# Keys of both head pairs first, then values 512 columns wide over two halves of the depth

## The reference

```
h_ctx = modulate(rms_norm(ctx), ...)             # 256 context tokens
h     = modulate(rms_norm(x), ...)               # 512 tokens
k_ctx, v_ctx = split(h_ctx @ w_in[:, 512:1536])  # 4 heads of 128
s_f = einsum('bhld,hl,bhle->bhde', k_ctx, w_f, v_ctx)   # decayed states, forward
s_b = einsum('bhld,hl,bhle->bhde', k_ctx, w_b, v_ctx)   # and backward
q, k, v, g, f = split(h @ w_in)                  # 512 columns each
q, k = rope(q), rope(k)
o = retention(q, k, v, forward, s_f) + retention(q, k, v, backward, s_b)
```

## Time and profile before

| | |
|---|---|
| time, median of 3 runs | 1349.7 us (1349.34 to 1349.88) |
| profiled execution, its own time | 1348.56 us |
| its span, first to last instruction | 1346.8 us |
| TensorE matmul busy | 1327.9 us, 99% of the span |
| VectorE busy | 901.4 us, 67% |
| ScalarE busy | 526.4 us, 39% |
| GpSimd busy | 83.8 us, 6% |
| 16 DMA engines, mean | 131 GB/s |
| granted TensorE clock, mean | 1.000 |

### The profile page before, as it was taken

One profiled execution on the slowest core, in us unless ns is written; L12 is line 12 of the kernel. 1 busy time (PEld: TensorE's weight loads), 2 busy tenths in 40 slices (PEclk: granted clock), 3 DMA queues, 4 the chain that ended last, 5 costly groups with the idle time before them and its releaser, 6 DMA issues.

```text
span 1346.8 us, 15738 instructions
## 1 busy us (share of the span) xinstructions
PE 1327.9 (99%) x6461; PEld 1077.6 (80%) x6461; DVE 901.4 (67%) x1126; ACT 526.4 (39%) x747; POOL 83.8 (6%) x148
## 2 busy tenths in 40 slices
PE   7999999999999999999999999999999999999998
PEld 4799688778888888887888777778878888888886
DVE  4787878988777777678758899766875433332224
ACT  4552444344334443222422666774333222222112
POOL 0000001000000001010000100000002220000000
PEclk9999999999999999999999999999999999999999
DMA  9543046324445555654123211112224332224331
GB/s 390 191 141 126 17 155 220 125 78 175 163 162 196 171 183 186 217 202 173 71 94 98 90 64 63 63 63 96 98 86 131 116 115 94 94 98 161 107 104 63
DMA packets 32887, 176.47 MB, mean 131 GB/s; under 512 B 4128, under 2 KB 4400, under 8 KB 17840
## 3 DMA queue, kind: packets, MB, share of 16 engines
q1 hardware_dynamic: 19440, 128.78, 26.7%
q0 software_dynamic: 13376, 46.69, 10.8%
HBM read 171.26 MB, written 4.20 MB: 130 GB/s over the span
## 4 chain that ended last, share of the span: by engine, by line
PE 90%; DVE 5%; issue 2%; ACT 2%; DMA 2%; SPq 0%; DVEq 0%; ACTq 0%
PE bank L1475 27%; PE bank L1477 26%; PE bank L1476 26%; PE bank L1814 2%; PE bank L1815 2%; PE bank L1820 2%; PE bank L1680 1%; DMA adaf<-ada 1%; PE bank L2010 1%; PE bank L1980 1%; DVE WL L830 1%; DVE sums L1174 1%; PE bank L1998 1%; PE bank L1997 1%; DMA raw<-weights 1%
## 5 line engine op out<-in xcount | busy, mean ns | idle before, releaser
L1475 PE MATMUL bank<-hH,WH 128*128 128x512 f32 x992 | 390.1, 393 | 0.9 <-DVE WL L830 0.6
L830 DVE TENSOR_TENSOR WL<-raw,WH 128x2048 fp32r<-128x2048 f32 x103 | 234.5, 2278 | 230.2 <-ACT WH L372 230.2
L1477 PE MATMUL bank<-hH,WL 128*128 128x512 f32 x992 | 386.4, 390 | 0.0
L1476 PE MATMUL bank<-hL,WH 128*128 128x512 f32 x992 | 386.2, 389 | 0.0
L372 ACT ACTIVATE WH<-raw 128x2048 fp32r<-128x2048 f32 x106 | 201.5, 1904 | 237.3 <-DMA raw<-weights 237.3
L1475 PEld LDWEIGHTS bank<-hH,WH 128*128 128x128 f32 x992 | 186.3, 188 | 42.6 <-issue 3.3
L1477 PEld LDWEIGHTS bank<-hH,WL 128*128 128x128 f32 x992 | 186.2, 188 | 39.6
L1476 PEld LDWEIGHTS bank<-hL,WH 128*128 128x128 f32 x992 | 186.3, 188 | 37.6 <-issue 0.2
L859 DVE SCALAR_TENSOR_TENSOR ada_acc<-ada_half,csil,ada_acc 128x1024 f32<-128x1024 f32 x70 | 89.7, 1281 | 6.4 <-DMA ada_half<-ada_later 3.8
L1307 DVE SCALAR_TENSOR_TENSOR cacc<-uT,vec,cacc 128x511 f32<-128x511 f32 (+29 forms) x120 | 83.3, 755 | 0.0
L335 POOL DMA_DIRECT2D ada_half<-ada_later x80 | 42.4, 530 | 571.8 <-DVE ada_acc L859 333.4
(11 more groups left out here) (333 smaller groups left out, 2075.1 us busy)
## 6 DMA issues: line engine op xcount, KB each, us to landing
raw<-weights SPq DMA_DIRECT2D x108, 1024.0 KB, 4.9
ada_half<-ada_later POOLq DMA_DIRECT2D x80, 512.0 KB, 4.4
adaf<-ada SPq DMA_DIRECT2D x8, 1024.0 KB, 19.8
xT<-x_t SPq DMA_DIRECT2D x4, 512.0 KB, 5.7
x_rows<-xB POOLq DMA_DIRECT2D x32, 64.0 KB, 2.2
x_tok<-x_rows POOLq DMA_DIRECT2D x1, 2048.0 KB, 10.9
out_t<-x_tok SPq DMA_DIRECT2D x8, 256.0 KB, 2.0
ctxT<-ctx_t SPq DMA_DIRECT2D x1, 1024.0 KB, 28.6
```

Source lines behind the costliest of these rows:

```text
L830: TT_(WL[:, slot, 0:width], raw[:, slot, 0:width], WH[:, slot, 0:width], sub).then_inc(s.lo_done, 1)
L1475: mm(o, lh, rh, start=start, stop=False, skip_group_check=skip)
L1476: mm(o, lh, rl, start=False, stop=False, skip_group_check=skip)
L1477: return mm(o, ll, rh, start=False, stop=stop, skip_group_check=skip)
```

## The change

Chunk order and layout: the four chunks after the queries were keys 0, values 0, keys 1, values 1. They are now keys 0, keys 1 and two chunks of values (`C_VALUES` and the next), each with all 512 value columns of one half of the depth (512 of the 1024 input rows). The values are therefore made with 512 moving columns: per token block 4 x 3 matmuls from the first chunk and 4 x 3 from the second into the same bank, in place of 2 pairs x 8 x 3 matmuls of 256 columns.

TensorE's new list: keys 0 (banks 6, 7), context keys 0 (banks 4, 5), keys 1 (banks 0, 1), context keys 1 (banks 2, 3), first half of the values (tokens into banks 6, 7, 4, 5, context into 0, 1), second half: context first, then token blocks 2 and 3, then `states(0)` into bank 0, then token blocks 0 and 1; then the retention loop, where `states(1)` goes into bank 1. Scores 0 and 1 now wait for the copies of token blocks 2 and 3 (`v_read`).

```
-                pe.wait_ge(s.rope_sum, HEADS)
-                states(0)
...
+            have(C_VALUES)
+            for t in range(TT):
+                pe.wait_ge(s.rope_sum, HEADS + t + 1) if t < 2 else pe.wait_ge(s.kc_scaled, t - 1)
+                value_part(0, VALUE_BANKS[t], hH, hL, t)
+            for tt in range(TC):
+                pe.wait_ge(s.rope_sum, HEADS + 2 + tt + 1)
+                ins = value_part(0, tt, hcH, hcL, tt)
+            ins.then_inc(s.mm_done, 16)
+            have(C_VALUES + 1)
+            for tt in range(TC):
+                value_part(1, tt, hcH, hcL, tt).then_inc(s.mm_done, step(tt, TC + TT))
+            for x, t in enumerate(VALUE_ORDER):
+                if x == 2:
+                    states(0)
+                value_part(1, VALUE_BANKS[t], hH, hL, t).then_inc(s.mm_done, step(TC + x, TC + TT))
...
+                    else:
+                        pe.wait_ge(s.v_read, i + 1)
...
-                    pe.wait_ge(s.state_lo, 1)
                     states(1)
                     pe.wait_ge(s.v_read, 4)
```

VectorE's new list (`context_keys` holds the same instructions per pair as before, `value_tile` is one copy of 128x512 in place of one of the four copies before):

```
+            rope_pair(0, KEY_BANKS[0], kH, kL, C_KV, 4, HEADS)
+            split_lo(C_VALUES)
+            context_keys(0)
+            rope_pair(1, KEY_BANKS[1], kH, kL, C_KV + 1, 4, HEADS)
+            split_lo(C_VALUES + 1)
+            ada_steps(2)
+            context_keys(1)
+            ada_steps(2)
+            for tt in range(TC):
+                dve.wait_ge(s.vc_hi, tt + 1)
+                TT_(vcL[:, tt, :], bank[tt][:, :], vcH[:, tt, :], sub).then_inc(s.vc_lo, 1)
+            dve.wait_ge(s.kc_lo, 4)
+            dve.wait_ge(s.places_in, 32)
+            decay_args(0)
+            split_lo(C_F)
...
+            ada_steps(2)
+            value_tile(0)
+            value_tile(1)
+            ada_steps(2)
+            states_lo(0)
+            value_tile(2)
+            value_tile(3)
```

More of the change, by code:

```diff
@@ L85 @@
 BAND = L + (TT - 1) * P
+KEY_BANKS, CONTEXT_BANKS, VALUE_BANKS = (6, 0), (4, 2), (6, 7, 4, 5)
+VALUE_ORDER = (2, 3, 0, 1)
+C_VALUES = C_KV + 2
 HALF, FOLD = L // 2, L // 2 + 2
@@ L115, in build @@
         rstd = fix("rstd", [P, L])
+        SCRATCH_AT = base[0]
         scratch = fix("scratch", [P, 2, L])
@@ L452, in states_hi @@
                 A(sH[:, :, 2 * p:2 * p + 2, :],
-                  bank[3][:, :].rearrange("p (d h e) -> p d h e", d=2, h=2), ACT.Copy).then_inc(s.state_hi, 1)
+                  bank[p][:, :].rearrange("p (d h e) -> p d h e", d=2, h=2), ACT.Copy).then_inc(s.state_hi, 1)
             def decays(h):
@@ L471, in _, with context_keys_hi @@
             A(csdH[:, :], csd_in[:, :], ACT.Copy).then_inc(s.csd_hi, 1)
[L473 to L480, removed]
+            def context_keys_hi(p):
                 for tt in range(TC):
                     act.wait_ge(s.kc_scaled, 2 * p + tt + 1)
[L483 to L490, removed]
+                    A(kcH[p][:, tt, :, :], kctmp[:, :, :], ACT.Copy).then_inc(s.kc_hi, 1)
+            rope_pair(0, KEY_BANKS[0], kH, C_KV, 4, HEADS)
+            split_hi(C_VALUES)
+            context_keys_hi(0)
+            rope_pair(1, KEY_BANKS[1], kH, C_KV + 1, 4, HEADS)
+            split_hi(C_VALUES + 1)
+            context_keys_hi(1)
+            for tt in range(TC):
+                act.wait_ge(s.mm_done, done(C_VALUES + 1, tt, TC + TT))
+                A(vcH[:, tt, :], bank[tt][:, :], ACT.Copy).then_inc(s.vc_hi, 1)
+            decays(0)
+            split_hi(C_F)
+            states_hi(0)
             def token_decays(h):
@@ L994, in _, with context_keys @@
             TT_(csdL[:, :], csd_in[:, :], csdH[:, :], sub).then_inc(s.csd_lo, 1)
[L995 to L1006, removed]
+            def context_keys(p):
                 for tt in range(TC):
-                    dve.wait_ge(s.mm_done, done(C_KV + 2 * p, 2 + tt, 4))
+                    dve.wait_ge(s.mm_done, done(C_KV + p, 2 + tt, 4))
                     if 2 * p + tt:
@@ L1016, in _, with value_tile @@
                     dve.wait_ge(s.kc_hi, 2 * p + tt + 1)
[L1017 to L1033, removed]
+                    TT_(kcL[p][:, tt, :, :], kctmp[:, :, :], kcH[p][:, tt, :, :], sub).then_inc(s.kc_lo, 1)
+            rope_pair(0, KEY_BANKS[0], kH, kL, C_KV, 4, HEADS)
[13 more added lines that the diff above has]
+            split_lo(C_F)
+            def value_tile(x):
+                t = VALUE_ORDER[x]
+                dve.wait_ge(s.mm_done, done(C_VALUES + 1, TC + x, TC + TT))
+                V.tensor_copy(vF[:, t, :], bank[VALUE_BANKS[t]][:, :]).then_inc(s.v_read, 1)
+            ada_steps(2)
[5 more added lines that the diff above has]
+            value_tile(3)
             def cross(h):
@@ L1593, in _, with states @@
                     turn(c)
+            def states(q):
+                pe.wait_ge(s.kc_lo, 2 * q + 2)
+                pe.wait_ge(s.vc_lo, TC)
+                for d in range(2):
+                    for h in range(2):
+                        at = slice(P * (2 * d + h), P * (2 * d + h) + P)
+                        hs, vs = slice(P * h, P * h + P), slice(256 * q + P * h, 256 * q + P * h + P)
+                        for tt in range(TC):
+                            ins = mm3(bank[q][:, at], kcH[q][:, tt, d, hs], kcL[q][:, tt, d, hs], vcH[:, tt, vs],
+                                      vcL[:, tt, vs], tt == 0, tt == TC - 1, True)
+                ins.then_inc(s.state_done, 1)
             for p in range(2):
-                slot, c = 0, C_KV + 2 * p
+                c = C_KV + p
                 have(c)
@@ L1600, in _ @@
                     if p:
-                        pe.wait_ge(s.rope_sum, HEADS + n + 1)
-                    project(bank[6 + n][:, :], c, n, hH, hL, ALL).then_inc(s.mm_done, step(n, 4))
+                        pe.wait_ge(s.rope_sum, n + 1)
+                    project(bank[KEY_BANKS[p] + n][:, :], c, n, hH, hL, ALL).then_inc(s.mm_done, step(n, 4))
                     if p == 0 and n == 0:
@@ L1606, in _ @@
                         mm(bank[4][:, 0:LC], ones[:, :], csqacc[:, :], start=True, stop=True).then_inc(s.stat_done, 1)
[L1608 to L1621, removed]
-                    pe.wait_ge(s.rope_sum, HEADS)
-                    states(0)
                 for tt in range(TC):
+                    if p:
+                        pe.wait_ge(s.rope_sum, 2 + tt + 1)
                     for k in range(KT):
@@ L1628, in _ @@
                         ts = slice(P * tt, P * tt + P)
-                        ins = mm3(bank[4 + tt][:, 0:256], hcH[:, k, ts], hcL[:, k, ts], wh, wl, k == 0, k == KT - 1)
+                        ins = mm3(bank[CONTEXT_BANKS[p] + tt][:, 0:256], hcH[:, k, ts], hcL[:, k, ts], wh, wl, k == 0, k == KT - 1)
                     ins.then_inc(s.mm_done, step(2 + tt, 4))
[L1632 to L1651, removed]
@@ new lines, in value_part @@
+            def value_part(half, b, src_h, src_l, t):
+                slot = (C_VALUES + half) % SLOTS
+                ts = slice(P * t, P * t + P)
+                for k in range(4):
+                    ws = slice(RET * k, RET * k + RET)
+                    ins = mm3(bank[b][:, :], src_h[:, 4 * half + k, ts], src_l[:, 4 * half + k, ts], WH[:, slot, ws],
+                              WL[:, slot, ws], half == 0 and k == 0, half == 1 and k == 3)
+                return ins
+            have(C_VALUES)
@@ L2098, in weight_stream @@
     for p in range(2):
-        put(C_KV + 2 * p, w_in, [col(2 + p, 256)])
-        put(C_KV + 2 * p + 1, w_in, [col(4 + p, 256)])
+        put(C_KV + p, w_in, [col(2 + p, 256)])
+        out[C_VALUES + p] = tiles(w_in[CW * p:CW * p + CW], [col(2, RET)]).reshape(P, CH)
         put(C_Q + p, w_in, [col(p, 256)])
```

11 lines of the change are left out of this document (7 added, 4 removed).

## The result

| | before | after |
|---|---|---|
| median of the runs | 1349.7 us (5 runs, 1347.61 to 1349.88) | 1355.87 us (5 runs, 1355.06 to 1357.21) |
| ratio to before, 95% interval | | 1.0051 (1.0037 to 1.0064) |
| profiled execution, span | 1348.56, 1346.8 | 1355.87, 1354.1 |
| granted clock, mean | 1.000 | 0.996 |

The change made the kernel slower by 0.51%, 6.9 us by the ratio (5.0 to 8.7) and 6.2 by the medians. The forecast was 3.4 us slower, 1353.1: the sign and the place were right, the size was half of what came. The measured 1355.87 lies at the upper end of the stated range, 1351.0 to 1356.0.

A forecast was written before the change was run, and what follows sets the result against it. TensorE, busy 99%, bounds the kernel, with VectorE close behind at the cross product. Terms -1.9 (wider values), -0.8 (wait gone), +4.8 (before scores 2), +1.5 (before cross product), gaps 0.2: 3.4 us slower, 1353.1, range 1351.0 to 1356.0.

The forecast's parts named there:

- the sign and the place: Slower by 3.4 us, with time lost before scores 2 and before the cross product, and none outside 71 to 136.
- VectorE's wait for `WH` of `C_F`: Behind `decay_args(0)`, VectorE idles from 114.7 to 117.5, 2.8 us, while ScalarE takes the decay's exponential and then `WH`.
- wait for step 7's load: VectorE at 123.5 waits 1.8 us for a load issued after step 5 is read, landing at 125.3.
- steps 7 and 8 with the transpose and the sum take 4.38, to 129.7: VectorE's steps ahead of the low part of states 0, priced from 118.61 to 122.99 in the trace before.
- the 6.2 of the earlier trace: Possible length of step 7's load if issued together with weights; result then 2.2 us later, 1355.3.
- The 4.0 of the earlier trace: Length taken for step 7's load, from two such loads in a row without weights.
- the clock: Rival: TensorE's clock falls to 1.2 GHz after its 4.8 us wait; price 0 to 2.4 us, 15% for 1 or more.
- the walk: Step-by-step timing of VectorE's and TensorE's lists, putting the cross product at 135.2 instead of 131.79, 3.4 us later.
- the worst of both: Case left out of the range, which reaches 1356.0 for the long load or the fallen clock.
- The double buffer is no wait: Rival: step 7's load lands by 123.5, so VectorE does not wait for it; 1351.3 us, 12%.
- The gain arrives: Rival: first score tile by 127.4 and states 1 by about 129, so TensorE keeps its 2.7 us; 1347.0, 13%.
- the wait for `WL` that goes: TensorE's 0.55 us wait at 89.11 for the second keys' chunk disappears, worth some 0.8 us in all.

The follow-up runs named there:

- e4: The changed kernel with SyncE's 1 MB weight load of chunk 8 issued only when step 8 has been read; 1354.48 us, ratio 1.0041 to before.
- e5: The changed kernel with its eight steps spread to where VectorE had idle time, none between the value copies; 1346.49 us, ratio 0.9984 to before.
- e6: e5 with each value product of 512 columns issued as two groups of 256, order kept; 1347.69 us, ratio 0.9994 to before.
- e7: The kernel before with only its steps moved, steps 1 and 2 one place later each; 1347.65 us, ratio 0.9991 to before.
- e1: The changed kernel with steps 5 to 8 called one place earlier on VectorE; 1351.54 us, ratio 1.0018 to before.
- e2: The changed kernel with 28 unread matmuls of 512 columns filling TensorE's idle stretch before scores 2; 1354.12 us, ratio 1.0041 to before.
- e8: The changed kernel with e4's later weight load and 21 of e2's unread matmuls; 1352.39 us, ratio 1.0034 to before.
- e3: The changed kernel with two ScalarE neighbours swapped, split_hi(C_F) ahead of decays(0); 1351.02 us, ratio 1.0015 to before.

## Why the prediction was right in place and wrong in size

**Right: the mechanism and its place.** VectorE's list and not TensorE's decides; the time is lost between scores 1 and the cross product. Step by step, forecast and measured (in the first profile, whose stretch starts 0.18 late):

| | forecast | measured |
|---|---|---|
| spacing of the wide values | 0.2267 | 0.227 |
| first values' chunk ready in time | by 0.5 | yes, no idle at 87.98 |
| scores 0 | 123.1, copies just hidden | 123.76, 0.20 of it a wait for the copies |
| VectorE's wait for `WH` of `C_F` | 2.8 | 2.82 |
| wait for step 7's load, step starts | 1.8, 125.3 | 1.72, 125.93 |
| wait for step 8's load | none | 2.33 |
| TensorE idle before scores 2 | 4.8 | 7.36 |
| cross product starts | 135.2 | 138.26 |
| and takes | 1.5 | 2.80 |

**Wrong: the term "steps 7 and 8 with the transpose and the sum take 4.38, to 129.7".** The row it came from had both loads in place. The term asks of two loads that they have landed, and I put a price and a range on one of them, step 7's, and left the other at nothing without naming the work that hid it. Step 8's load took 8.7 us, and from the start of step 7 to the low part of the states it measured 6.82 (125.93 to 132.75), of which 2.33 are the wait. I had seen that the weights are issued at 123.1, and laid them beside step 7's load, which landed after 3.7 all the same; they lay beside step 8's, issued 0.3 us ahead of them. e4 shows that this is the cause: without the weights beside it the load took 4.7 and the wait was gone.

To name the load would not have been enough. With the 6.2 of the earlier trace rows, the row that I called nearest, issued at about 122.7 by the prediction's steps, it would have landed at 128.9, and step 8's multiplication was due at 129.0: still no wait. But the trace of the kernel before has the same pattern, a second load of this kind with weights issued less than 1 us behind it, at several places: at 349.18 it took 6.8, at 403.58 6.4, and at 204.21 8.4. GpSimd's issue, SyncE's, and the time to landing of the last:

```profile
204.21 0.53 POOL L335 DMA_DIRECT2D ada_half<-ada_later  x1 [1.10 <-DVE ada_acc L859]
```

```profile
205.15 0.33 SPq L303 DMA_DIRECT2D raw<-weights  x1
```

```profile
ada_half<-ada_later POOLq DMA_DIRECT2D x1, 512.0 KB, 8.4
```

From that row VectorE would have waited some 2 us for step 8's load, and the sum would have been 1355 or so (an estimate: 122.7 + 8.4 = 131.1 against 129.0). The 4.0 of the earlier trace rows was read loosely too: it is the median of two loads, 3.7 for the first, which is step 7's place, and 4.3 for the second.

**Wrong in its chance: the clock.** I gave the fall 15% and a price of up to 2.4. It fell in both profiles of the changed kernel and in e4, whose wait of 4.87 us is the one I had forecast. So for a wait of that length it should have been the forecast. The price was 1.29 in the first profile and 0.3 in the second. The Trainium skill, "TensorE: Matmul & The Clock Gate", section "What's actually happening", states that an array left idle falls to half clock; the prediction put this rule aside because no stretch of the trace showed it, but the trace had no wait as long between two matmuls either, and so said nothing against it. These runs agree with the page: the clock is at 0.50 behind waits of 4.06 to 7.36 us. The trace of the kernel before even had a hint: its first four matmuls of 508 columns, behind 4.20 us without any, take 3.56 us from 4.20 on, and the same four take 1.95 at 15.06. Its granted clock reads 1.00 at both places, and what made the first ones slow is not shown.

**The sum of the first profile**: 3.44 of the walk + 2.33 + 1.29 are 7.06 of 7.58; the rest, 0.5, is VectorE's delay of 0.4 by step 7 (0.29 of it a wait for step 4's load, which was also issued beside a weight load) and small gaps. The ratio of all runs says 6.9. The range left out "the worst of both", a long load and a fallen clock. Both came, the long load being step 8's and not step 7's.

**The rivals.** "The double buffer is no wait" did not come: step 7 waited 1.72. "The gain arrives" did not come either, but had the right size of the gain, 2.7 against e5's 2.5, and the right condition: a first score tile by 127.4. e5 meets it (its first tile is done at 126.54 + 0.68, in a profile whose stretch starts 0.96 late). The gain has two parts: 1.4 by the width (e5 against e6) and 0.8 by the wait for `WL` that goes (e7); the remaining 0.3 I have not tested.

## What to carry to other kernels

Where filler work with a double buffer is moved, each piece needs two questions: does the engine have idle time there, and were the last two pieces long enough ago that its load is there, with what else the DMA engines carry at that time? Price every load that a moved group waits for, not only the first, and take the longest row of such a load in the whole trace, not the nearest: beside a load of twice its size one of 512 KB mostly took 6.0 to 9.3 us here, without it 3.6 to 5.1. And a wait on the bounding engine that is longer than any in the trace is priced twice, for its length and for the clock behind it.

## What the runs showed of the hardware

- In the stretch of the change, over all profiles, a load of 512 KB from GpSimd's queue landed after 3.6 to 4.0 us when no other was under way and after 4.0 to 5.1 when one of its kind had been issued less than 2 us before it. With a 1 MB weight load of SyncE's queue issued within 0.5 us of it, it took 6.0 to 9.3 us in 14 of 16 cases (6.2 and 8.7 in the changed kernel's first profile, 8.7 in e1, 7.8 in e2, 9.3 in e7, where nobody waited for it). The other two, issued 0.46 us ahead of the weights with no load under way, took 3.7 (e4) and 3.9 (e8). What makes one of the fourteen 6 and another 9 is not shown. The 1 MB load beside it took 5.4 to 9.0.
- TensorE's granted clock stayed at 1.00 through a wait of 2.40 us in e3's profile and fell to 0.50 in waits of 4.06 (e1), 4.87 (e4) and 7.3 (the changed kernel, twice).
- The start of the program scatters by itself. In e1's profile the stretch began at 77.23, 6.2 us late, though nothing ahead of it was changed; its windows show the clock at a half for part of the first 35 us, in which TensorE waits often and briefly:

```profile
20.00:25.00 5.00, 4.40 (x26) 0.67 1.02 429
25.00:30.00 5.00, 4.50 (x25) 0.50 1.01 428
30.00:35.00 5.00, 5.00 (x38) 0.80 1.01 426
```

The kernel before has 1.00 in the same windows. In e6's profile the window 20 to 25 shows 0.67 and the stretch begins 1.5 late. I had not expected this. The late start is 6.2 of the 9 us by which e1's profiled execution lies above the one of the kernel before. Single executions of e1 lie up to 10 us apart (1347.7 to 1357.9), and how much of that the start makes in the others is not shown. A comparison of profiles from a common mark leaves it out.
